# Two output blocks of a weight slab computed together, row tile by row tile, where a matrix product starts on inputs still being made

## What is computed

```python
def rmsnorm(x, g):
    y = xf * lax.rsqrt(jnp.mean(xf * xf, axis=-1, keepdims=True) + EPS)
    return (y * g.astype(jnp.float32)).astype(x.dtype)
...
    hn = rmsnorm(h, ffn_norm[i])
    h = h + jnp.square(jax.nn.relu(hn @ ffn_w1[i])) @ ffn_w2[i]
    gate = jax.nn.sigmoid(rmsnorm(h, ple_norm[i]) @ ple_w_gate[i])
    h = h + gate * (p[i] @ ple_w_proj[i])
```

## Time and profile before

| | |
|---|---|
| runs | 2306.33, 2306.70, 2308.54 us; median 2306.7 |
| span of the profiled execution | 2308.7 us, 27336 instructions |
| its own time | given only as this span; the nearest of the three runs is 2308.54 |
| TensorE matmul busy | 2153.5 us, 93% |
| VectorE, ScalarE, POOL busy | 1154.3 (50%), 791.1 (34%), 939.4 us (41%) |
| mean granted TensorE clock | 0.971 |
| DMA | 196.74 MB, mean 85 GB/s |

### The profile page before, as it was taken

One profiled execution on the slowest core, in us unless ns is written; L12 is line 12 of the kernel. 1 busy time (PEld: TensorE's weight loads), 2 busy tenths in 40 slices (PEclk: granted clock), 3 DMA queues, 4 the chain that ended last, 5 costly groups with the idle time before them and its releaser, 6 DMA issues.

```text
span 2308.7 us, 27336 instructions
## 1 busy us (share of the span) xinstructions
PE 2153.5 (93%) x10068; PEld 1764.5 (76%) x10068; DVE 1154.3 (50%) x1624; ACT 791.1 (34%) x1044; POOL 939.4 (41%) x306
## 2 busy tenths in 40 slices
PE   7547999999999999999999998999899999999997
PEld 6445788888878987778888876777777878888885
DVE  5996543233473545462342557328444357445364
ACT  5445422122442146321221344324225243222232
POOL 4785344344343420334444342343253334434332
PEclk9878999999999999999999999999999999999998
DMA  4121222322322211222222321132220222322231
GB/s 178 37 73 55 91 91 93 108 91 91 106 77 93 101 46 36 100 73 98 103 91 93 107 89 58 55 114 73 73 92 1 92 91 91 109 92 91 92 108 55
DMA packets 30717, 196.74 MB, mean 85 GB/s; under 512 B 4384, under 2 KB 4512, under 8 KB 7984
## 3 DMA queue, kind: packets, MB, share of 16 engines
q1 hardware_dynamic: 30640, 195.68, 24.4%
HBM read 193.54 MB, written 2.13 MB: 85 GB/s over the span
## 4 chain that ended last, share of the span: by engine, by line
issue 43%; PE 38%; POOL 13%; DVE 5%; ACT 1%; POOLq 0%; ACTq 0%; DVEq 0%
PE gp L490 11%; PE gp L492 11%; PE gp L491 11%; POOL w_lo L366 11%; PE ms L692 2%; PE gp L644 2%; POOL pool_sum L422 2%; PE ms L629 1%; DVE T L1602 1%; DVE T L1146 1%; DVE U L1601 1%; DVE xc L1149 0%; DVE U L1146 0%; DVE U L1447 0%; DVE merged L1146 0%
## 5 line engine op out<-in xcount | busy, mean ns | idle before, releaser
L366 POOL TENSOR_TENSOR w_lo<-raw,w_hi 128x2048 fp32r<-128x2048 f32 x176 | 813.3, 4621 | 1192.9 <-ACT w_hi L786 1187.4
L490 PE MATMUL gp<-a_hi,w_hi 128*128 128x512 f32 x1440 | 572.4, 397 | 56.9 <-DVE T L1146 27.2
L491 PE MATMUL gp<-a_lo,w_hi 128*128 128x512 f32 x1440 | 566.0, 393 | 0.0
L492 PE MATMUL gp<-a_hi,w_lo 128*128 128x512 f32 x1440 | 565.9, 393 | 0.0
L490 PE MATMUL gp<-b_hi,w_hi 128*128 128x512 f32 (+1 forms) x1216 | 476.0, 391 | 41.3 <-POOL b_lo L434 27.4
L786 ACT ACTIVATE w_hi<-raw 128x2048 fp32r<-128x2048 f32 x175 | 333.5, 1906 | 436.0 <-PE gp L492 431.2
L491 PE MATMUL gp<-b_lo,w_hi 128*128 128x512 f32 (+1 forms) x1216 | 472.6, 389 | 0.0
L492 PE MATMUL gp<-b_hi,w_lo 128*128 128x512 f32 (+1 forms) x1216 | 472.4, 389 | 0.0
L490 PEld LDWEIGHTS gp<-a_hi,w_hi 128*128 128x128 f32 x1440 | 274.2, 190 | 121.8 <-DVE T L1146 28.0
L491 PEld LDWEIGHTS gp<-a_lo,w_hi 128*128 128x128 f32 x1440 | 274.2, 190 | 58.6 <-issue 2.0
L492 PEld LDWEIGHTS gp<-a_hi,w_lo 128*128 128x128 f32 x1440 | 273.7, 190 | 57.8
(11 more groups left out here) (255 smaller groups left out, 2100.4 us busy)
## 6 DMA issues: line engine op xcount, KB each, us to landing
raw<-w_hbm SPq DMA_DIRECT2D x176, 1024.0 KB, 4.9
fbias<-negc_scratch SPq DMA_DIRECT2D x16, 256.0 KB, 3.1
h<-x_hbm SPq DMA_DIRECT2D x4, 512.0 KB, 7.1
out_hbm<-h SPq DMA_DIRECT2D x4, 512.0 KB, 2.7
mem_raw<-mem_hbm SPq DMA_DIRECT2D x1, 1024.0 KB, 12.1
p_raw<-p_hbm SPq DMA_DIRECT2D x2, 512.0 KB, 9.1
par<-par_hbm SPq DMA_DIRECT2D x1, 264.5 KB, 5.2
wga<-w_a_hbm SPq DMA_DIRECT2D x2, 64.0 KB, 2.3
```

Source lines behind the costliest of these rows:

```text
L366: g.tensor_tensor(w_lo[:, s], raw[:, s], f32(w_hi[:, s]), ALU.subtract).then_inc(w_lo_done, 1)
L490: pe.matmul(o, wh, xh, start=start, stop=False)
L491: pe.matmul(o, wh, xl, start=False, stop=False)
L492: return pe.matmul(o, wl, xh, start=False, stop=stop)
```

## The change

In a first slab with `ready`, both banks are now waited for first. Then, row tile by row tile, `slab_ws` waits for the tile's low part and issues the three matmuls of block 0 and the three of block 1. Both blocks so end together (block 0 three matmuls before block 1), and the hook is called behind both. Slabs without `ready` and the other engines' programs are unchanged.

```diff
@@ -496,6 +496,20 @@
                 s = sp_.slot(2)
                 cc = 16 // kk
                 pe.wait_ge(w_lo_done, sp_.at(1))
+                if ready is not None and cc == 2:
+
+                    banks = [free_bank(bp, c) for c in range(2)]
+                    for k in range(kk):
+                        pe.wait_ge(lo_done, ready.at(k + 1))
+                        for c in range(2):
+                            at = (2 * k + c) * P
+                            m = three(gp[:, banks[c], 0:n], w_hi[:, s, at:at + P], w_lo[:, s, at:at + P],
+                                      x[0][:, k0 + k, 0:n], x[1][:, k0 + k, 0:n], k == 0, k == kk - 1)
+                            if k == kk - 1:
+                                m.then_inc(blk_done, 1)
+                    if hook:
+                        hook()
+                    return
                 for c in range(cc):
                     b = free_bank(bp, c)
                     for k in range(kk):
```

## The result

| | before | after |
|---|---|---|
| median of the runs | 2306.61 us (4 runs, 2306.33 to 2308.54) | 2329.55 us (4 runs, 2326.81 to 2333.54) |
| span of the profiled execution | 2308.7 us | 2331.7 us (its own time 2333.54) |
| mean granted TensorE clock in it | 0.971 | 0.965 |

The change makes the kernel slower: the ratio of after to before is 1.0096, with a 95% interval from 1.0081 to 1.011. The difference of the medians is +22.9 us and that of the two spans +23.0 us; the forecast was +17.3, and 2329.55 lies within the range of 2312 to 2334.

A forecast was written before the change was run, and what follows sets the result against it. TensorE was taken as the bound, where only its gaps and clock can change; 6.6 + 3.0 + 0 + 0.3 + 7.9 - 0.5 + 0 = +17.3 us on the median 2306.7 gave 2324.0 us, range 2312 to 2334.

The forecast's parts named there:

- The sign, the mechanism and the places: Slower: later `stat` delays the third slab's `w_lo`, so TensorE waits in `ffn[0]`, both gates and `ffn2`, then half clock.
- `ffn[0]`: Third slab's `w_lo` late: TensorE waits 4.0 us and loses 2.6 us to half clock, 6.6 us in all.
- The other new waits: Waits for `w_lo` at the third slabs of `gate[0]`, `gate[1]` and `ffn2`, each over 5 us.
- about 31: TensorE's waits for `w_lo` over the whole kernel were to grow from 11.4 to about 31 us.
- `gq`: Starts some 6.6 us late, gives part back, second slab 2.8 us late; `gate[0]` and `gq` together +3.0 us.
- `gate[1]` and `gqx`: Late `w_lo` in the gate plus half clock, nearly all given back in `gqx`: +0.3 us.
- the first product: `stat` moves from 22.5 to 26.5, but the convolution, bound by VectorE, ends where it ended: zero.
- the down products: The 11 down slabs have no wait inside their first block, so nothing is gained there.
- `ffn[1]`: Nothing changes: the moved `stat` is still ahead of VectorE's `var`, and the wait of 4.55 us stays.
- `ffn2`: Third slab's `w_lo` late: a wait of 5.3 us plus 2.6 of clock, 7.9 us.
- `pw2`: Pairs end at 238.5, but the second slab's `w_lo` limits the gain to 0.5 of 2.3 us: -0.5.
- a rival of 2339 us: Evictions bite: 22 slabs each lose 0.69 us, 15.2 us on top of the forecast, 2339.2 us; chance 0.02.

The follow-up runs named there:

- third experiment: The change, but with the hook called after 24 matmuls, as before it, in `ffn[0]`, `ffn[1]`, the gates and `ffn2`: 2301.12 us, ratio 0.9963.
- fourth experiment: The change, but ScalarE makes the third slab's `w_hi` ahead of `rstd` (feed-forward layers, gates, `ffn2`) and later gate weights a block earlier: 2288.5 us, ratio 0.9921.
- eighth experiment: The kernel before the change, with pairs of blocks only in `gq` and `gqx`: 2298.17 us, ratio 0.9962.
- fifth: The kernel before the change, without pairs, with only ScalarE's early weights added: 2296.81 us, ratio 0.9956.

## Why the prediction was right, and where its sizes were off

The sign, the mechanism and the places were right. Term by term, with the profiles of before and after cut at the same matmul:

- *`ffn[0]`* +6.6, forecast 4.0 + 2.6; measured: the third slab starts 3.95 late (idle 3.78), and half clock adds 2.6. Moving the hook back (third experiment) or the weights ahead (fourth) took it to 0: shown, not only argued.
- *The other new waits*: 4.99, 5.62 and 5.38 us for 5.2, 5.4 and 5.3. The total of 31.4 us for `w_lo` is the "about 31" of the forecast.
- *`gq`* gave back as the prediction described: it started 6.7 us late against its own past (forecast 6.6), `stat` came 7.8 us late, and its second slab was held by `w_lo`. But the two stages came to +4.5 and not +3.0. The second slab started 2.7 us late, for 2.8 forecast; the term that is missing is half clock behind its wait of 1.23 us, from 710.9 to 714.3, and it makes 1.8 us. The prediction put no price on a wait below 3 us. Here too chance has a part: of the other seven kernels with pairs in `gq`, where the same wait is 1.21 to 1.39 us, one had half clock behind it (the third experiment) and six had none.
- *`gate[1]` and `gqx`* -0.1 for +0.3, *the first product* +0.3 for 0, *the down products* 0.00.
- *`ffn[1]`* kept its wait, 4.57 for 4.55 us. Its -1.1 us are half clock that lasted 3.4 and not 5.8 us.
- *`ffn2`* +6.8 for +7.9: the wait was right, the clock's part was 1.4 us and not 2.6. In `gate[0]` and `gate[1]` it was 2.8 and 2.1.
- *`pw2`* is the term furthest off: -0.5 forecast, +2.4 measured. The pairs ended at 237.8 (238.5 was forecast) and the second slab started 0.5 us earlier, as forecast; but I took that gain as net. The wait of 2.79 us in front of it was followed by half clock from 240.6 to 246.7, which cost 3.0 us. The term that was left out is the clock behind a gap that the change itself opens. Whether that clock falls is not settled by the program: three other kernels had the same wait (2.74 to 2.75 us) at full clock, among them the fourth experiment, and there this stage came to -0.4, which is the forecast; with a wait of 1.8 us it was +1.2 twice.
- *Elsewhere* +3.7 us, in steps of 1.1 to 1.6 us up and down, where I had 0: half clock in `wo` behind attention (6.8 us for 3.4), and between the cross attention and `wout` other ones of the same waits were followed by half clock (2.01 us at 1536.63 and 2.37 at 1741.54 in the change, their like of 1.99 and 2.40 before were not; 1.41 us at 1455.23 before was, its like was not). The same steps come and go in experiments that leave those stages' programs alone, so no mechanism of the change is shown for them.
- *The own time* of a profiled execution is 1.8 us over its span in every run where both are given. So the profile before stood some 3.9 us above the median and not 2.0. It doesn't enter the sum, which is a difference.

Together the terms that missed by over 1 us are the clock's: +2.9 in `pw2`, +1.5 in `gate[0]` and `gq`, +3.7 in places that I had at 0, -1.1 in `ffn[1]`, -1.1 in `ffn2`, together 5.9 us, where the whole miss is 23.0 - 17.3 = 5.7. So the waits were forecast well, and that the total came out within 6 us owes something to luck: the clock's terms move by as much from one execution to the next. The prediction set a rival of 2339 us beside what the Trainium skill says (Perfetto Trace Analysis, Matmuls): that groups should rotate through banks, so that the eviction of one lies beside the next one's matmuls. No loss from two groups open together shows here: 14 slabs of that kind measured 1.0008. In `ffn[0]` of the change VectorE emptied the pair's two banks by 294.92, and the slab that needs them next started at 302.77.

The gain that the change was capable of is real, 9 to 10 us in `gq` and `gqx` (eighth experiment). The change got 6.9 us of it, and the four hooks of `ffn[0]`, both gates and `ffn2` took 24.6.

## What to carry to other kernels

When an instruction is moved on one engine, list all that stands behind its consumers on the other in-order engines, not only its consumers: here a reduction moved by 5.44 us held up weights that need nothing of it. Work that depends only on loads belongs ahead of such a chain in its engine's order; that alone was worth 11 us before the change and turned its +22.9 into -19.1. Interleave blocks only where inputs really lag, and price a gap of TensorE at more than its length: in these profiles the half clock behind a wait of 3.8 to 5.6 us cost another 1.4 to 2.8 us, and that behind a shorter one nothing or up to 3.

## What the runs showed of the hardware that was not expected

The same wait leaves half clock of different lengths: 3.4 or 5.8 us behind 4.57 and 4.55 us of waiting in `ffn[1]`. Each of the waits for low weights of 3.78 us and more was followed by half clock, in every profile. Short gaps do it sometimes: 1.23 us in `gq` and 2.79 us in `pw2` did in the changed kernel, 1.37 and 2.75 us at the same two places in the fourth experiment did not, and 1.99 us did not. The wait of 3.07 us in front of `wout` was followed by half clock in the profile before; in five of the experiments, two of them (the fifth and eighth) with that stage's program as it was, `wout` was 2.7 us shorter. Such steps are a likely cause of the spread of single runs, up to 7 us within one kernel: in the third experiment the fastest run (2296.14 us) had a mean granted clock of 0.976 and the slowest (2302.95) one of 0.972, though which steps they had was not followed. And a pass of POOL over 128 x 2048 values can stretch a subtraction of VectorE from 0.69 to 3.77 us. This isn't special to that experiment: in the change an operation of VectorE on `U<-T` in `ffn[0]` took 3.52 us, started inside POOL's pass of 298.20 and ended 0.56 us behind it.
